# A conditioned hybrid decoder layer on one core: the start of the kernel re-ordered (who issues the small inputs, how the first w_ada tile is stored, in which pieces the last x tile is scaled)

## The reference, cut to what matters

```python
mod = jax.nn.silu(c) @ w_ada + b_ada                    # c: one vector of 1024, w_ada: 1024 x 3072
shift, scale, gate = jnp.split(mod, 3, axis=-1)
h = rmsnorm(x, g_norm) * (1.0 + scale[:, None, :]) + shift[:, None, :]     # x: 512 x 1024
proj = h @ w_in                                         # w_in: 1024 x 4096
q, k, v, z_attn, b_g, c_g, h_c, z_conv = jnp.split(proj, splits, axis=-1)
q, k = rope(q, positions), rope(k, positions)
y_attn = rmsnorm(moba_attention(q, k, v), g_attn_out) * silu(z_attn)
y_conv = rmsnorm(short_gated_conv(b_g, c_g, h_c, w_conv), g_conv_out) * silu(z_conv)
y = concat([y_attn, y_conv]) @ w_out
return rmsnorm(x + gate * y, g_final)
```

## Time and profile before

| what | value |
|---|---|
| median of 3 runs | 277.91 us (277.49 to 278.29) |
| the profiled execution | 278.23 us, of which the span of the records is 276.4 us |
| TensorE (PE) busy | 262.3 us, 95% of the span |
| VectorE (DVE) busy | 206.9 us, 75% |
| ScalarE (ACT) busy | 136.2 us, 49% |
| GpSimd (POOL) busy | 113.1 us, 41% |
| share of the chain that ended last | PE 90%, ACT 2%, DMA 2%, issue 2% |
| in from HBM | 38.85 MB |

### The profile page before, as it was taken

The page is one execution under the profiler, slowest core; times in us unless marked ns, Lnnn a source line. Parts: engine busy times, 40 slices in busy tenths (PEclk is TensorE's granted clock), DMA queues, the critical chain, the costliest instruction groups (busy, mean ns, idle before and its releaser), DMA issues.

```text
span 276.4 us, 3680 instructions
## 1 busy us (share of the span) xinstructions
PE 262.3 (95%) x1278; PEld 215.0 (78%) x1278; DVE 206.9 (75%) x334; ACT 136.2 (49%) x228; POOL 113.1 (41%) x69
## 2 busy tenths in 40 slices
PE   5689999999999999999999999999999999999990
PEld 1367888888888888888888888887888888888880
DVE  4697887589999985969969675924595554896774
ACT  5676556447158545393544723546835764001342
POOL 2500000373806433075366322337667948451330
PEclk9999999999999999999999999999999999999998
DMA  5999963596812561119573111632832535500024
GB/s 196 361 418 415 414 256 105 197 349 180 246 68 88 155 167 62 63 68 338 184 176 100 58 70 76 154 76 77 262 120 76 199 106 171 210 0 2 38 115 152
DMA packets 12212, 45.38 MB, mean 164 GB/s; under 512 B 2081, under 2 KB 2593, under 8 KB 10786
## 3 DMA queue, kind: packets, MB, share of 16 engines
q1 hardware_dynamic: 11906, 44.89, 47.7%
q10 hardware_dynamic: 288, 0.26, 0.3%
HBM read 38.85 MB, written 2.10 MB: 148 GB/s over the span
## 4 chain that ended last, share of the span: by engine, by line
PE 90%; ACT 2%; DMA 2%; issue 2%; SPq 1%; POOL 0%; DVE 0%; POOLq 0%
PE ps L1017 22%; PE ps L1019 21%; PE ps L1018 21%; PE ps L1077 5%; PE ps L1162 4%; PE ps L1152 3%; PE ps L1140 3%; DMA xt<-in_x 2%; PE ps L1092 2%; PE ps L1098 2%; PE ps L1090 2%; PE ps L1096 2%; PE ps L1051 1%; ACT x_junk L313 1%; PE ps L1085 1%
## 5 line engine op out<-in xcount | busy, mean ns | idle before, releaser
L590 POOL TENSOR_TENSOR w_lo<-raw,w_hi 128x1024 fp32r<-128x1024 f32 x29 | 74.5, 2582 | 111.4 <-ACT w_hi L334 72.0
L1017 PE MATMUL ps<-h_lo,w_hi 128*128 128x512 f32 x200 | 79.2, 396 | 0.0
L1019 PE MATMUL ps<-h_hi,w_hi 128*128 128x512 f32 x200 | 78.0, 390 | 0.0
L1018 PE MATMUL ps<-h_hi,w_lo 128*128 128x512 f32 x200 | 78.0, 390 | 0.0
L1019 PEld LDWEIGHTS ps<-h_hi,w_hi 128*128 128x128 f32 x200 | 37.5, 188 | 7.9
L1017 PEld LDWEIGHTS ps<-h_lo,w_hi 128*128 128x128 f32 x200 | 37.5, 188 | 7.9
L1018 PEld LDWEIGHTS ps<-h_hi,w_lo 128*128 128x128 f32 x200 | 37.6, 188 | 7.5
L334 ACT ACTIVATE w_hi<-raw 128x1024 fp32r<-128x1024 f32 x29 | 30.1, 1051 | 3.2 <-DMA raw<-in_wslots 3.2
L405 ACT ACTIVATE probs<-probs,rmin 128x384 f32<-128x384 f32 (+3 forms) x32 | 17.5, 550 | 14.7 <-DVE rmin L824 14.7
L712 DVE CUSTOM_DVE_ANT_0 mod_junk<-ada,c_bc,prm 128x1024 f32<-128x1024 f32 x15 | 23.1, 1542 | 1.1
L834 DVE TENSOR_SCALAR probs<-probs,prec 128x384 f32<-128x384 f32 (+3 forms) x32 | 20.7, 709 | 0.3
(11 more groups left out here) (145 smaller groups left out, 477.1 us busy)
## 6 DMA issues: line engine op xcount, KB each, us to landing
raw<-in_wslots SPq DMA_DIRECT2D x33, 512.0 KB, 3.4
ada<-in_ada SPq DMA_DIRECT2D x11, 1024.0 KB, 8.0
raw<-in_whead SPq DMA_DIRECT2D x8, 448.0 KB, 7.3
xt<-in_x SPq DMA_DIRECT2D x4, 512.0 KB, 5.4
qd<-qt SPq DMA_DIRECT2D x16, 128.0 KB, 2.4
kd<-kt SPq DMA_DIRECT2D x16, 128.0 KB, 2.4
x<-in_x SPq DMA_DIRECT2D x4, 512.0 KB, 5.7
out<-x SPq DMA_DIRECT2D x3, 512.0 KB, 2.7
```

What stands on the lines that cost most here:

```text
L590: nc.gpsimd.tensor_tensor(lo, src[:, :], hi.bitcast(F32), ALU.subtract).then_inc(s_lo, 1)
L1017: nc.tensor.matmul(o, a_hi, b_lo, start=start, stop=False)
L1018: nc.tensor.matmul(o, a_lo, b_hi, start=False, stop=False)
L1019: return nc.tensor.matmul(o, a_hi, b_hi, start=False, stop=stop)
```

## The change

Four edits, all in the head. (1) The loads of `crow`, `posi` and `prm` are issued by ScalarE's queue, ahead of its SiLU, and no longer by SyncE ahead of the x tiles. (2) The two halves of the first w_ada tile are stored as an array of their own (`ada0`), so that each half is one contiguous 512 KB block in HBM; before, a half was 128 rows of 4 KB, each 8 KB from the next. (3) The last x tile is scaled in two pieces: columns 0 to 127 first, the other 896 columns after `h_hi` of chunk 0. (4) The copy `sin_t` is moved ahead of the wait for the last 1/rms, the sine's transposes wait for the sine alone, and one `keep_warm` of 256 columns is dropped.

```diff
-            sp.dma_start(crow[0:1, :], c).then_inc(c_in, 16)
-            sp.dma_start(posi[:, :], pos).then_inc(pos_in, 16)
-            sp.dma_start(prm[:, :], prm_d).then_inc(prm_in, 16)
             for m in range(TT):
                 sp.dma_start(xt[:, m, :], x[m * P:(m + 1) * P, :]).then_inc(x_in[m], 16)
             for two in range(2):
-                sp.dma_start(ada[0][:, two, :], ada_d[0, :, two, :]).then_inc(a0_in[two], 16)
+                sp.dma_start(ada[0][:, two, :], ada0_d[two]).then_inc(a0_in[two], 16)
...
         def _(act):
+            nc.scalar.dma_start(crow[0:1, :], c).then_inc(c_in, 16)
+            nc.scalar.dma_start(posi[:, :], pos).then_inc(pos_in, 16)
+            nc.scalar.dma_start(prm[:, :], prm_d).then_inc(prm_in, 16)
             act.wait_ge(c_in, 16)
...
             square_x(3)
-            act.wait_ge(x_rstd, TT)
-            nc.scalar.activation(xt[:, TT - 1, :], xt[:, TT - 1, :], ACT.Copy, scale=rstd[:, TT - 1:TT]).then_inc(x_norm3, 1)
             act.wait_ge(trig_tr, 1)
             nc.scalar.activation(sin_t[:, :], bank(2), ACT.Copy, scale=prm[:, C_SIGN:C_SIGN + 1]).then_inc(trig_ok, 1)
+
+            def scale_last_x(lo, hi):
+
+                nc.scalar.activation(xt[:, TT - 1, lo:hi], xt[:, TT - 1, lo:hi], ACT.Copy, scale=rstd[:, TT - 1:TT]
+                                     ).then_inc(x_norm3, 1)
+
+            act.wait_ge(x_rstd, TT)
+            scale_last_x(0, P)
...
                 if j == 0:
+                    scale_last_x(P, D)
+                    act.wait_ge(trig_tr, 2)
                     nc.scalar.activation(cos_t[:, :], bank(3), ACT.Copy).then_inc(trig_ok, 1)
...
-            pe.wait_ge(trig_k, 2)
-            for b, src in ((2, sin_k), (3, cos_k)):
+            for n, (b, src) in enumerate(((2, sin_k), (3, cos_k))):
+                pe.wait_ge(trig_k, n + 1)
                 for m in range(TT):
                     ins = nc.tensor.transpose(bank(b, m * P, (m + 1) * P), src[:, m, :], ident[:, :])
-            ins.then_inc(trig_tr, 1)
+                ins.then_inc(trig_tr, 1)
...
                         else:
-                            keep_warm(2 * P)
                             pe.wait_ge(x_norm3, 1)
+                    if j == 1 and m == TT - 1:
+                        pe.wait_ge(x_norm3, 2)
```

More of the change, by code:

```diff
@@ L42, in two_pi_pieces, with build @@
     return pieces
-def build(nc, x, c, pos, prm_d, ada_d, whead_d, wslots_d, gfin_d, out):
+def build(nc, x, c, pos, prm_d, ada0_d, ada_d, whead_d, wslots_d, gfin_d, out):
     S, D = x.shape
@@ L242, in load_ada @@
                     sp.wait_ge(mod_step, 2 * ((j - 4 if j < 10 else j - 2) + 1))
-                sp.dma_start(dst[:, :, :], ada_d[j]).then_inc(arrived, 16)
-            sp.dma_start(crow[0:1, :], c).then_inc(c_in, 16)
-            sp.dma_start(posi[:, :], pos).then_inc(pos_in, 16)
-            sp.dma_start(prm[:, :], prm_d).then_inc(prm_in, 16)
+                sp.dma_start(dst[:, :, :], ada_d[j - 1]).then_inc(arrived, 16)
             for m in range(TT):
@@ L1305, in host_layout @@
     return [("x", v["x"][0]), ("c", v["c"]), ("pos", np.ascontiguousarray(v["positions"].reshape(4, P).T)),
-            ("prm", prm), ("ada", ada), ("whead", whead), ("wslots", np.ascontiguousarray(np.stack(slots))),
+            ("prm", prm), ("ada0", np.ascontiguousarray(ada[0].transpose(1, 0, 2))), ("ada", ada[1:]), ("whead", whead), ("wslots", np.ascontiguousarray(np.stack(slots))),
             ("gfin", v["g_final"])]
```

## The result

The change makes the kernel slower: 281.85 us median (280.91 to 282.55, six runs) against 278.1 (277.49 to 278.63, six runs), ratio 1.0135 with a 95% interval of 1.0118 to 1.0153. The profiled execution took 281.39 us against 278.23 before. Forecast were 277.0 and a range of 276.3 to 278.1.

What follows compares the result with a forecast made beforehand. Chunk 1's start was taken to decide the time, with TensorE dense afterwards. Earlier `h_lo` (-0.94) plus late `prm` (+0.05) gave -0.9 us: 277.3 from the profiled 278.23, 277.0 by median; range 276.3 to 278.1.

Steps and rivals of the forecast that it cites:

- The frame: TensorE is dense after the head, so the change acts only through chunk 1's start, then at 22.05 us.
- the ring: ScalarE-VectorE loop feeding TensorE: 4.91 us per chunk against TensorE's 5.40; chunk 1 starts when both are ready.
- The landings of x: x tiles in the head: issue 1.29 us earlier, landings move by -1.2 us after sharing with small inputs.
- The step "given back": 896 columns between `h_hi` and float32 copy: 0.95 us more, leaving `h_lo` -0.94 of the -1.9 at the first product.
- the landing of `prm`: Start of VectorE's angle chain: `prm` in at 4.15, bounds 3.6 (nothing in its way) and 5.5; costs +0.05 us.
- The bad end of my sum: Every term at its bad bound, with `prm` landing at 4.7: gain of only 0.3 us.
- The chain behind it: VectorE's angles (4.63 us), three scalings and two reductions (2.2 + 2.7): shift no earlier than `prm` landing + 9.7 us.
- the rival "small inputs come late": ScalarE's queue served behind x tiles: `prm` at 5.5, shift 15.2, +0.5 us or 278.4; chance 0.20.
- the clock, at 0.05: TensorE's clock rises late: a whole chunk 0 at the lower level ends at +2.3 us, 280; chance 0.05.
- otherwise 0: Dropped `keep_warm` gives TensorE room ahead of tile 3's transpose; no other effect, apart from the clock rival.
- The price per late product: TensorE's chunk 0: a late clock rise costs about 0.2 us per product of 0.23; first 0.6 us free.
- The halves: First w_ada tile's halves stored apart: same bytes, VectorE arrives from tile 2's scaling; 0, bounds 0 and -0.2 us.

Runs made afterwards that it cites:

- e8: Kernel before with only the split scaling of the last x tile and the moved copies: 278.27 us, ratio 1.0006.
- e10: Changed kernel with prm and posi first on SyncE, crow alone on ScalarE, the thrown-away product back, 896 columns behind the float32 copy: 276.94 us, ratio 0.9964.
- e2: Kernel before with only crow, posi and prm issued by ScalarE's queue: 280.76 us, ratio 1.0101.
- e1: Changed kernel with crow, posi and prm issued by SyncE ahead of the x tiles again: 279.06 us, ratio to before 1.0037.
- e7: Kernel before with only the thrown-away 256-column product ahead of the last x tile's transpose dropped: 279.18 us, ratio 1.0032.
- e3: Changed kernel with the thrown-away 256-column product ahead of the last x tile's transpose put back: 280.82 us, ratio to before 1.0105.
- e4: Kernel before with only the two halves of the first w_ada tile stored apart: 277.75 us, ratio 0.9988.
- e5: Changed kernel with ScalarE's three issues in the order prm, posi, crow: 279.28 us, ratio to before 1.0042.
- e12: Changed kernel with the positions packed into prm as four more columns, so posi's 128 small rows go: 278.75 us, ratio to before 1.0027.

## Why the prediction was wrong

**The frame held.** The start of chunk 1, the later of the ring and TensorE, decides the time to 0.1 us in thirteen of fourteen profiles. The issue of x, the shift as the new release of `h_hi`, and the 0.93 us of the 896 columns came as worked out. The landings of x did not: tile 2's square began 2.0 us earlier and not 1.2 (7.46 against 9.47), which `prm` made worthless. The step "given back" was right in kind: e8 shows no gain, e10 gets it back.

**The step that failed is the one on the angle chain: the landing of `prm`.** I put it at 4.15 with bounds of 3.6 and 5.5, "near the free bound", because it is a tenth of an x tile. It landed at 7.6. The bad end of my sum did not even use the bound of 5.5, but 4.7. The chain behind it was right within 0.4 (landing + 9.3 is the shift, where I had 9.7; my own terms, 4.63, 2.2 and 2.7, add up to 9.5), and so was the sign of the rival "small inputs come late"; only its bound was wrong. I took "behind x tile 1" as the worst. But `prm` stood behind `posi` too, and the two together are 288 small packets beside those of x; they took 3.4 us to pass instead of 0.9, and started some 1.5 us late besides. I had weighed bytes where the packets count. e2, the queue alone, carries +2.66 us of the +3.75 by median (+1.99 in its profile).

The rule of the Trainium skill that I had set beside the sum, page "DMA: Bandwidth & Descriptors", section "Queues, rings and completion order" (an engine takes turns between queues, packet by packet), agrees with the trace: 286 small packets beside 324 of the other queue in 3.4 us. With the packets spread evenly over the core's 16 DMA engines, that is an estimated 0.2 us for each small packet of an engine. I had called the rule's result "somewhere between the bounds". The count could have been made from the rows: an x tile of 128 rows took 1.3 us, 8 rows for each of 16 engines, so 0.16 us a row; the 16 small rows of an engine, each behind one of x, are 2.6 us on top of the free landing. That estimate puts `prm` at 6.2, beyond the 5.0 where the gain was nil, and speaks against the change.

**The second failure is the clock, at 0.05.** I held against it that TensorE would work from 4.5 to 13 with hardly a gap. It had a gap of 2.67 us before the sine, because `prm` was late. But that gap is not what did it: the kernel before had one of 2.64 there, and e1 and e7, where `prm` was in at 3.6 and 4.8, are slow as well with gaps of 1.78 and 1.51 (1.33 and 1.83 us between ring and TensorE). The dropped product is enough: +1.10 us by e7, and -1.0 by e3 when it is put back. I had entered it as "otherwise 0". The price per late product was right.

**The halves** were put at 0 with a bound of -0.2; they gave 0.35 us (0.0 to 0.6), which the interval barely sets apart from nothing.

Taken one by one, on medians, the four edits give +2.66 (queue, e2), +1.10 (dropped product, e7), +0.19 (split, e8) and -0.35 (halves, e4): +3.60, against +3.75 measured together. The last two terms are at the edge of what the runs can tell.

## What to carry to other kernels

Ask of a small transfer who waits for it and count its packets. Here a table of 128 short rows on a second queue, beside the 512 KB loads of x, saw about one large packet pass for each of its own; issued ahead of them on their own queue it cost them some 0.4 us of issue. Small tables that can be packed into one should be. A product whose result nobody reads was worth 1 us ahead of the first dense stretch: before removing it, look at whether the engine's clock is up where its work begins. Work moved "behind" a critical result is free only if it is also moved behind the next one that the ring needs.

## What the runs showed of the hardware that was not expected

- `prm`, 48 KB in 128 rows, took 1.8 to 3.2 us from issue to landing with the x loads behind it on its own queue, and 4.0 (issued first, e5) to 6.2 us (issued third, e3) beside x loads of the other queue. Part of this is a later start of the small packets: 2.6 us after the issue of `posi` in the changed kernel, 1.0 before.
- The granted clock rose at very different moments for small differences in TensorE's work: ahead of chunk 0 or at its start with two thrown-away 256-column products; in the middle of chunk 0, by the spacing of its products at about 20.7 to 22.6 us, with one (e1, e7, the changed kernel, with gaps of 1.78, 1.51 and 2.67 us before the sine); and ahead of it again with one where the work before had no gap or a short one (e5; e12's profile, with a gap of 1.06 us). The Trainium skill's page "TensorE: Matmul & The Clock Gate", section "What's actually happening", calls the lower level the default that activity releases; these rows agree. These are single profiles, so whether the gap decides it is not shown. The times spread by 0.2 us over six runs in e5, where the clock was up, and by 1.9 over eight in e7.
- The last x tile landed 6.2 to 7.3 us after its issue with the small inputs ahead on the same queue, and 6.0 to 6.7 with all of them on the other. The two ranges overlap, so whether the queue is the reason for the pause at tile 2 stays open. The strided rows are not, by e4.
